# Joining small TensorE products in the head loop of a hybrid transformer layer

## The chip, the cores and the metric

One Trainium2 chip, one core of it. The metric is the time of one execution of the whole program on the device, in microseconds (us); of several runs the median is given. One layer is computed, with all of its weights read from HBM.

## The reference, cut to what matters

The change lies in the three attention-like mixers. For 256 tokens and 8 heads of 128 channels the reference computes:

```python
proj = rms_norm(x) @ w_in                      # q, k, v of three mixers, gates
# A: sliding window with sinks ("sw")
scores = einsum('qd,kd->qk', q, k) * d ** -0.5      # over the window
e = exp(scores - max(scores, sink)); probs = e / (sum(e) + exp(sink - m))
out_a = probs @ v
# B: stick breaking ("sb")
z = q @ k.T
a = exp(log_sigmoid(z) + between)              # between: a reverse cumulative sum
out_b = a @ v
# C: gated DeltaNet ("dn"), chunks of 64
n_mat = -strict_lower(kbeta @ k.T * decay)
t_mat = eye + n_mat; power = n_mat
for _ in range(5):
    power = power @ power
    t_mat = t_mat + t_mat @ power
```

Behind it come gated sums of the three, an output product, a mixture of 32 experts and a gated input embedding.

## The kernel before, in words

**Dense work.** Every weight matrix is split into a high and a low part of type fp32r, and each product is the sum of three: high by high, high by low, low by high. In the head stage a tile of 128 columns of the input projection is 48 matmuls (`tile`, L494, its matmul is L509); `dense` (L532) runs a quarter of it, 12 matmuls. ScalarE (ACT) makes the high part (`hi`), VectorE (DVE, `lo`, L1349, recorded as L1352) the low part of even tiles and GpSimd (POOL, `lo_pieces`, L459, four pieces each, recorded as L463) that of odd tiles, once ACT has made the high part.

**Heads.** `mix` is written once for each engine (TensorE: PE, L542; ACT, L1089; DVE, L1438) and runs for heads 1 to 8. It interleaves the small fp32 products of head n with 32 pieces of dense work, which are head n+1's projection (in head 8: the first gate products, fp32r matmuls of 512 columns, L713). Between two pieces stands one group of small products; the program order on each engine is written out by hand, and semaphores tie the engines. The groups that matter here, all on PE:

- L554 `dn_ss`, then one dense piece, then L558 `sw_ss` (a sum of squares over the channels for the sliding window's q), which waits for `dn_rt`, ACT's reading of the L554 result in the same bank; two dense pieces; then L564 and L565 `sb_z` (stick-breaking scores).
- L587 and L588 `sw_s` (sliding window scores) behind dense(9); L592 to L594 `sb_arg` (stick-breaking cumulative sums) behind dense(10); L599 `dn_p` behind dense(11).
- L604 `sw_prT` (three transposes of the sliding window's probabilities) behind dense(12).
- rounds r = 0 to 5 of the matrix power (L613 to L618 and L623, products of 64 by 64 blocks), one behind each of dense(13) to dense(18); the last matmul of that dense piece is held until DVE's `dn_round` and ACT's `dn_roundp` of the round before. Behind round 0 stands `sw_av` (L628, L629), behind round 1 `sb_av` (L634, L635), the products of probabilities and values.

ACT between them: `sw_rt` after `hi(2)`; three exponentials after `sw_max`; `Exp` of `am` after `sb_amin`; `evac(2)`; copies of `dn_p` into `pm` and `n21`; the copy of `sw_prT` into `pT`; `hi(5)`; then the copies of the rounds. DVE: the scan for `sb_sp` (L1463, L1466), the sliding window's mask and maximum (L1470 to L1475, gives `sw_max`), the decayed products and `dn_round` (L1479 to L1489), the cap of `sb_arg` (L1491, `sb_amin`), the normalization (L1493 to L1498, `sw_pr`), `lo(4)`, then for each round the copies L1503 and L1505 (`dn_round`), and behind rounds 0 to 3 a tap of head n+1's convolution (`next_tap`: L1423, a copy of 12 columns, and three instructions at L1428 in the first tap, L1430 in the others). Head 8 has no taps and no POOL work, and its `lo(3)` is a real subtraction (L1547); in heads 1 to 7 `lo(3)` is empty.

Of the kernel before, what the change touches and what calls it, by code (L numbers as in the profile page):

```python
# [18 lines left out]
ALU = mybir.AluOpType  # L19
# [63 lines left out]
def hybrid_trunk(nc, x, p, mix_norm, w_in, swa_q_norm, swa_k_norm, swa_sinks, sb_q_norm, sb_k_norm, dn_conv,  # L83
# [3 lines left out]
    with ctx:  # L87
# [28 lines left out]
        def event(name, n):  # L116

            name, before = base.get(name, (name, 0))
            return sem(name), n + before
# [355 lines left out]
        def _(pe):  # L475
# [66 lines left out]
            def mix(m, n, dense):  # L542
# [5 lines left out]
                for t in range(TT):  # L548
# [5 lines left out]
                mm(bank[5][:], ones[:], sq_dn, start=True, stop=True).then_inc(sem("dn_ss"), 1)  # L554
                dense(5)
                pe.wait_ge(*event("dn_rt", n))
                pe.wait_ge(*event("sw_sq", n))
                mm(bank[5][:, 0:S], ones[:], sq_sw, start=True, stop=True).then_inc(sem("sw_ss"), 1)  # L558
                dense(6)
                dense(7)  # L560

                pe.wait_ge(*event("sb_qk", n))
                kk = qk_sb[:, S:2 * S]
                mm(bank[3][:, 0:S], kk[:, 0:P], qk_sb[:, 0:S], start=True, stop=False, skip_group_check=True)  # L564
                mm(bank[3][:, S:S + P], kk[:, P:S], qk_sb[:, P:S], start=False, stop=False, skip_group_check=True)\  # L565
                    .then_inc(sem("sb_z"), 1)
                dense(8)

# [14 lines left out]
                dense(9)  # L583

                pe.wait_ge(*event("sw_q", n))
                kT = kT_sw[:, ds(m // 4, 1), :].rearrange("p a s -> p (a s)")
                mm(bank[4][:, 0:P], q_sw[:, 0:P], kT[:, 0:P], start=True, stop=True)  # L587
                mm(bank[4][:, P:3 * P], q_sw[:, P:S], kT[:, 0:S], start=True, stop=True).then_inc(sem("sw_s"), 1)  # L588
                dense(10)

                pe.wait_ge(*event("sb_sp", n))
# [9 lines left out]
                dense(12)  # L601
                pe.wait_ge(*event("sw_pr", n))
                for b in range(3):
                    m_ = pe.transpose(bank[4][:, b * P:b * P + P], smx[:, b * P:b * P + P], ident[:])  # L604
                m_.then_inc(sem("sw_prT"), 1)

                for r in range(6):
# [16 lines left out]
                    m_.then_inc(sem("dn_sqr"), 1)  # L624
                    if r == 0:
                        pe.wait_ge(*event("sw_pT", n))
                        pe.wait_ge(*event("sb_v", n))
                        mm(bank[2][:, 0:S], v_sw[:, 0:P], pT[:, 0:S], start=True, stop=False, skip_group_check=True)  # L628
                        mm(bank[2][:, P:S], v_sw[:, P:S], pT[:, S:3 * P], start=False, stop=True, skip_group_check=True)\  # L629
                            .then_inc(sem("sw_av"), 1)  # L630
                    if r == 1:
                        pe.wait_ge(*event("sb_a", n))
                        pe.wait_ge(*event("sw_out", n))
                        mm(bank[2][:, S:2 * S], v_sb[:, 0, :], am[:, 0:S], start=True, stop=False, skip_group_check=True)  # L634
                        mm(bank[2][:, S + P:2 * S], v_sb[:, 1, :], am[:, S:3 * P], start=False, stop=True,  # L635
                           skip_group_check=True).then_inc(sem("sb_av"), 1)
# [372 lines left out]
        def _(act):  # L1009
# [79 lines left out]
            def mix(n, evac, hi, sigmoid_conv):  # L1089
# [49 lines left out]
                f(n21[BLOCKS[1], :, :], nT_psum[BLOCKS[1], :, 0:CH], ACT.Copy).then_inc(sem("dn_n21"), 1)  # L1139
                act.wait_ge(*event("sw_prT", n))  # L1140
                f(pT, bank[4][:, 0:384], ACT.Copy).then_inc(sem("sw_pT"), 1)
                hi(5)
                for r in range(5):
                    act.wait_ge(*event("dn_sqr", 6 * n - 5 + r))
                    f(pm, pm_psum, ACT.Copy).then_inc(sem("dn_roundp"), 1)
                    if r == 0:
                        act.wait_ge(*event("sw_av", n))
                        f(outs[:, 0, ds(n - 1, 1), :].rearrange("p a s -> p (a s)"), bank[2][:, 0:S], ACT.Copy)\
                            .then_inc(sem("sw_out"), 1)
                    if r == 3:  # L1150
# [4 lines left out]
                    if r == 2:  # L1155
                        evac(3)
                        act.wait_ge(*event("sb_av", n))
                        f(outs[:, 1, ds(n - 1, 1), :].rearrange("p a s -> p (a s)"), bank[2][:, S:2 * S], ACT.Copy)\
                            .then_inc(sem("sb_out"), 1)
# [160 lines left out]
        def _(dve):  # L1320
            tt, ts, stt = dve.tensor_tensor, dve.tensor_scalar, dve.scalar_tensor_tensor

            def nxt():

                dve.drain()  # L1325
# [112 lines left out]
            def mix(n, next_tap, next_silu, lo):  # L1438
# [29 lines left out]

                dve.wait_ge(*event("sw_s", n))
                tt(smx, bank[4][:, 0:384], masksw[:].rearrange("p b n -> p (b n)"), ALU.add)  # L1470
                nxt()
                dve.tensor_reduce(sm[:, 0:1], smx[:, 0:P], AX.X, ALU.max)
                dve.tensor_reduce(sm[:, 1:2], smx[:, P:3 * P], AX.X, ALU.max)
                nxt()
                ts(sm[:, 2:4], sm[:, 0:2], hs[:, F_SINK:F_SINK + 1], -1.0, ALU.max, ALU.mult).then_inc(sem("sw_max"), 1)  # L1475

                dve.wait_ge(*event("dn_dec", n))
# [10 lines left out]
                dve.wait_ge(*event("dn_eg", n))  # L1488
                tt(eG, eG, qk_dn[:, P:S], ALU.mult).then_inc(sem("decays_used"), 1)  # L1489
                dve.wait_ge(*event("sb_arg", n))  # L1490
                tt(am, bank[3][:, 0:384], capsb[:].rearrange("p b n -> p (b n)"), ALU.min).then_inc(sem("sb_amin"), 1)  # L1491
# [341 lines left out]
```

## Time and profile before

| | us |
|---|---|
| median of 3 runs | 2133.97 |
| lowest and highest | 2130.94, 2138.09 |
| the profiled execution's own time | 2128.3 |
| its span in the trace | 2126.6 |
| PE busy in the span | 1796.1 (84%) |
| DVE, ACT, POOL busy | 864.0, 691.1, 191.2 |
| mean granted TensorE clock | 0.944 |

The profiled execution is one run with the profiler on; its span runs from the first to the last instruction in the trace. A busy PE is not PE at its peak, since the records of pipelined matmuls overlap: a matmul's record is longer than the distance to the next one's start, so distances between starts tell what a piece costs.

### The profile page before, as it was taken

To read this page: it belongs to the slowest core of one execution; us is meant where nothing else is said; L and a number is where in the kernel's file an instruction comes from. 1 tells how busy PE (TensorE), PEld (TensorE's weight loads), DVE (VectorE), ACT (ScalarE), POOL (GpSimd) and SP (SyncE) were. 2 spreads that over 40 slices of the span, in tenths; PEclk is the share of its full clock that TensorE was granted. 3 is DMA by queue.
4 is the path that set the end of the run, shared out by engine and by line. 5 is a ranking of instruction groups with operands and counts; after the bars stand their busy time and mean duration, and the time that the engine had idled before them with its cause. 6 is when DMAs were issued, how large, how long until landed. Compare 5 with 4: busy or idle time off the path is not lost.

```text
span 2126.6 us, 42236 instructions
## 1 busy us (share of the span) xinstructions
PE 1796.1 (84%) x17850; PEld 1354.2 (64%) x17851; DVE 864.0 (41%) x1392; ACT 691.1 (32%) x954; POOL 191.2 (9%) x167
## 2 busy tenths in 40 slices
PE   7999999999999999998977776666666666666699
PEld 7899999999878888887753443333333333333477
DVE  4555445554464445444433332222222222222274
ACT  4466655566654434333320111100011010110173
POOL 3433233223100000000000000000000000000000
PEclk9999999999999999999989998888888999988899
DMA  9555545454445555556759999999999999999972
GB/s 180 152 134 138 133 126 135 119 137 128 131 157 191 186 197 191 188 195 240 279 208 426 425 425 427 427 425 425 427 428 427 426 425 427 427 426 426 425 279 87
DMA packets 258914, 593.01 MB, mean 279 GB/s; under 512 B 31530, under 2 KB 171050, under 8 KB 225322
## 3 DMA queue, kind: packets, MB, share of 16 engines
q1 hardware_dynamic: 258858, 592.19, 74.7%
q8 instruction: 43, 0.70, 0.1%
q14 instruction: 13, 0.11, 0.0%
HBM read 590.07 MB, written 2.10 MB: 278 GB/s over the span
## 4 chain that ended last, share of the span: by engine, by line
PE 58%; DMA 34%; ACT 3%; DVE 2%; issue 1%; DVEq 1%; ACTq 1%; SPq 0%
DMA ring<-in_w_e_down 33%; PE bank L713 22%; PE bank L509 16%; PE bank L899 5%; PE bank L957 4%; PE bank L872 2%; ACT ring L1011 1%; PE bank L616 1%; ACT L1011 1%; PE bank L858 1%; PE bank L918 1%; PE bank L849 1%; DVEq L1325 1%; DMA ring<-in_w_out 0%; ACT wh L1011 0%
## 5 line engine op out<-in xcount | busy, mean ns | idle before, releaser
L1011 ACT ACTIVATE wh<-ring 128x2048 fp32r<-128x2048 f32 x156 | 298.3, 1913 | 218.9 <-DMA ring<-in_w_in 99.3
L872 PE MATMUL bank<-ring,mo 128*32 128x128 f32 x6144 | 216.4, 301 | 134.0 <-DMA ring<-in_w_e_up 114.1
L1011 ACT ACTIVATE mo<-bank 128x128 f32<-128x128 f32 (+5 forms) x232 | 72.5, 323 | 711.9 <-PE bank L886 308.9
L872 PEld LDWEIGHTS bank<-ring,mo 128*32 128x32 f32 x6144 | 187.8, 121 | 177.7 <-DMA ring<-in_w_e_up 143.7
L1547 DVE TENSOR_TENSOR wl<-ring,wh 128x2048 fp32r<-128x2048 f32 x86 | 197.0, 2292 | 218.2 <-ACT wh L1011 218.2
L899 PE MATMUL bank<-ring,mo 128*32 128x512 f32 x1024 | 163.5, 768 | 93.1 <-DMA ring<-in_w_e_down 87.3
L463 POOL TENSOR_TENSOR wl<-ring,wh 128x512 fp32r<-128x512 f32 x132 | 171.7, 1333 | 342.9 <-ACT wh L1011 342.9
L509 PE MATMUL bank<-xh,wh 128*128 128x256 f32 x1088 | 162.4, 296 | 3.0 <-ACT xh L1011 3.0
L1715 DVE TENSOR_TENSOR x_tok<-x_tok,bank 128x512 f32<-128x512 f32 x256 | 158.3, 680 | 0.0
L509 PE MATMUL bank<-xl,wh 128*128 128x256 f32 x1088 | 154.1, 289 | 0.0
L899 PEld LDWEIGHTS bank<-ring,mo 128*32 128x32 f32 x1024 | 33.8, 125 | 187.0 <-DMA ring<-in_w_e_down 97.1
L509 PE MATMUL bank<-xh,wl 128*128 128x256 f32 x1088 | 149.0, 286 | 2.5 <-DVE wl L1352 2.5
L509 PEld LDWEIGHTS bank<-xh,wh 128*128 128x128 f32 x1088 | 139.7, 193 | 11.4 <-issue 5.7
L509 PEld LDWEIGHTS bank<-xl,wh 128*128 128x128 f32 x1088 | 139.9, 193 | 1.2
L509 PEld LDWEIGHTS bank<-xh,wl 128*128 128x128 f32 x1088 | 137.1, 191 | 5.3 <-DVE wl L1352 2.9
L1725 DVE COPY mo<-bank 128x512 f32<-128x512 f32 x32 | 22.1, 692 | 242.2 <-PE bank L858 242.2
L1739 DVE TENSOR_TENSOR mo<-mo,bank 128x128 f32<-128x128 f32 x32 | 9.2, 288 | 269.1 <-PE bank L872 269.1
L1011 ACT ACTIVATE raw_dn<-bank 128x512 f32<-128x512 f32 (+1 forms) x56 | 28.0, 500 | 255.3 <-PE bank L899 248.6
L1011 ACT ACT_TABLE_LOAD x66 | 84.7, 1283 | 48.1 <-issue 43.1
L713 PE MATMUL bank<-wh,xh 128*128 128x512 f32 x384 | 97.2, 392 | 0.0
L713 PE MATMUL bank<-wl,xh 128*128 128x512 f32 x384 | 96.8, 391 | 0.0
L713 PE MATMUL bank<-wh,xl 128*128 128x512 f32 x384 | 96.7, 392 | 0.0
(354 smaller groups left out, 2350.4 us busy)
## 6 DMA issues: line engine op xcount, KB each, us to landing
ring<-in_w_e_down SPq DMA_DIRECT2D x64, 2048.0 KB, 26.2
ring<-in_w_e_up SPq DMA_DIRECT2D x64, 2048.0 KB, 26.2
ring<-in_w_in SPq DMA_DIRECT2D x116, 1024.0 KB, 5.5
ring<-in_w_e_gate SPq DMA_DIRECT2D x32, 2048.0 KB, 30.3
xnT<-in_w_e_gate SPq DMA_DIRECT2D x16, 2048.0 KB, 29.6
mo<-in_w_e_gate SPq DMA_DIRECT2D x16, 2048.0 KB, 33.9
ring<-in_w_out SPq DMA_DIRECT2D x16, 1024.0 KB, 5.2
ring<-in_w_ple_gate SPq DMA_DIRECT2D x8, 2048.0 KB, 15.1
```

The source lines that it names most:

```text
L463: i = pool.tensor_tensor(wl[p][:, k:k + 4, :], slot[p][:, k:k + 4, :], wh[p][:, k:k + 4, :], ALU.subtract)
L509: m = mm(to, w_[:, k, :], x_[:, k, :], start=(i == 0), stop=(i == len(steps) - 1))
L616: m_ = mm(pow_psum[rows_, t, :, :], pm[rows_, t, :], powT[rows_, t, :, :], start=True, stop=True)
L713: m = mm(to[t][:], x_(k0 + k, t), w_[p][:, k, :], start=(first and j < 8 and k == 0), stop=(last and j >= 16 and k == 3))
L849: m = mm(bank[4 + j][:], swT[32 * j:32 * j + 32, t, :], ysb[32 * j:32 * j + 32, :], start=True, stop=True)
L872: m = mm(bank[b][32 * j:32 * j + 32, 0:P], xw[:, 8 * (i % 2) + k, :], m_gu[piece][:, k, j * P:j * P + P], start=(i % 2 == 0 and k == 0), s ...
L899: m = mm(bank[3][32 * j:32 * j + 32, :], hT[:, 32 * c:32 * c + 32], m_down[i][:, 0, a, j * 512:j * 512 + 512], start=(c == 0), stop=(c == 3))
L957: m = mm(bank[ACC_BANK[u // 2] + t][:], x_[:, 8 * (u % 2) + k, t * P:t * P + P], w_[:, k, :], start=(first and k == 0), stop=(last and k = ...
L1011: return act.activation(out, in_, func, **kw)
L1547: tt(ul[u % PAIRS], unit_slot[u % PAIRS], uh[u % PAIRS], ALU.subtract).then_inc(sem("u_lo"), 1)
L1715: i = tt(o, o, bank[4 + j][:], ALU.add)
L1725: dve.tensor_copy(xg, bank[0][:]).then_inc(sem("xg"), 1)
```

## The change

It moves four of the small groups so that each stands directly beside another one, with no dense piece between, and moves what consumes them on ACT and DVE: `sw_ss` stands one dense piece later, `sb_z` one earlier, together; `sw_s` stands one dense piece later, in front of `sb_arg`; `sw_prT` moves from behind dense(12) to behind round 0; `sw_av` moves from behind round 0 to behind round 1, in front of `sb_av`. The wait for `sw_out` goes, both outputs are copied behind round 2, and the second product of the shared bank has `start=False`. On DVE the mask and maximum move behind the decayed products. Nothing is computed otherwise than before.

```diff
@@ -553,17 +553,16 @@
                 pe.wait_ge(*event("sb_rt", n))
                 mm(bank[5][:], ones[:], sq_dn, start=True, stop=True).then_inc(sem("dn_ss"), 1)
                 dense(5)
+                dense(6)
                 pe.wait_ge(*event("dn_rt", n))
                 pe.wait_ge(*event("sw_sq", n))
                 mm(bank[5][:, 0:S], ones[:], sq_sw, start=True, stop=True).then_inc(sem("sw_ss"), 1)
-                dense(6)
-                dense(7)
-
                 pe.wait_ge(*event("sb_qk", n))
                 kk = qk_sb[:, S:2 * S]
                 mm(bank[3][:, 0:S], kk[:, 0:P], qk_sb[:, 0:S], start=True, stop=False, skip_group_check=True)
                 mm(bank[3][:, S:S + P], kk[:, P:S], qk_sb[:, P:S], start=False, stop=False, skip_group_check=True)\
                     .then_inc(sem("sb_z"), 1)
+                dense(7)
                 dense(8)
 
                 pe.wait_ge(*event("dn_qk", n))
@@ -582,12 +581,12 @@
                 m_.then_inc(sem("dn_kk"), 1)
                 dense(9)
 
+                dense(10)
+
                 pe.wait_ge(*event("sw_q", n))
                 kT = kT_sw[:, ds(m // 4, 1), :].rearrange("p a s -> p (a s)")
                 mm(bank[4][:, 0:P], q_sw[:, 0:P], kT[:, 0:P], start=True, stop=True)
                 mm(bank[4][:, P:3 * P], q_sw[:, P:S], kT[:, 0:S], start=True, stop=True).then_inc(sem("sw_s"), 1)
-                dense(10)
-
                 pe.wait_ge(*event("sb_sp", n))
                 mm(bank[3][:, 0:S], negL[:], sp[:, 0:S], start=False, stop=False, skip_group_check=True)
                 mm(bank[3][:, P:S], nones[:], sp[:, S:S + P], start=False, stop=False, skip_group_check=True)
@@ -599,11 +598,6 @@
                     m_ = pe.transpose(nT_psum[:, t, :], nT[:, t, :], ident[:])
                 m_.then_inc(sem("dn_p"), 1)
                 dense(12)
-                pe.wait_ge(*event("sw_pr", n))
-                for b in range(3):
-                    m_ = pe.transpose(bank[4][:, b * P:b * P + P], smx[:, b * P:b * P + P], ident[:])
-                m_.then_inc(sem("sw_prT"), 1)
-
                 for r in range(6):
                     dense(13 + r, lambda: (pe.wait_ge(*event("dn_round", 6 * n - 5 + r)),
                                            pe.wait_ge(*event("dn_roundp", 6 * n - 5 + r))))
@@ -623,15 +617,18 @@
                                 m_ = mm(pm_psum[rows_, t, :], w_, pm[rows_, t, :], start=True, stop=True)
                     m_.then_inc(sem("dn_sqr"), 1)
                     if r == 0:
+                        pe.wait_ge(*event("sw_pr", n))
+                        for b in range(3):
+                            m_ = pe.transpose(bank[4][:, b * P:b * P + P], smx[:, b * P:b * P + P], ident[:])
+                        m_.then_inc(sem("sw_prT"), 1)
+                    if r == 1:
                         pe.wait_ge(*event("sw_pT", n))
                         pe.wait_ge(*event("sb_v", n))
                         mm(bank[2][:, 0:S], v_sw[:, 0:P], pT[:, 0:S], start=True, stop=False, skip_group_check=True)
                         mm(bank[2][:, P:S], v_sw[:, P:S], pT[:, S:3 * P], start=False, stop=True, skip_group_check=True)\
                             .then_inc(sem("sw_av"), 1)
-                    if r == 1:
                         pe.wait_ge(*event("sb_a", n))
-                        pe.wait_ge(*event("sw_out", n))
-                        mm(bank[2][:, S:2 * S], v_sb[:, 0, :], am[:, 0:S], start=True, stop=False, skip_group_check=True)
+                        mm(bank[2][:, S:2 * S], v_sb[:, 0, :], am[:, 0:S], start=False, stop=False, skip_group_check=True)
                         mm(bank[2][:, S + P:2 * S], v_sb[:, 1, :], am[:, S:3 * P], start=False, stop=True,
                            skip_group_check=True).then_inc(sem("sb_av"), 1)
                 dense(19, lambda: (pe.wait_ge(*event("dn_T", n)), pe.wait_ge(*event("dn_n21", n))))
@@ -1137,16 +1134,13 @@
                 f(pm[BLOCKS[0], :, :], nT_psum[BLOCKS[0], :, 0:CH], ACT.Copy)
                 f(pm[BLOCKS[1], :, :], nT_psum[BLOCKS[1], :, CH:P], ACT.Copy).then_inc(sem("dn_roundp"), 1)
                 f(n21[BLOCKS[1], :, :], nT_psum[BLOCKS[1], :, 0:CH], ACT.Copy).then_inc(sem("dn_n21"), 1)
-                act.wait_ge(*event("sw_prT", n))
-                f(pT, bank[4][:, 0:384], ACT.Copy).then_inc(sem("sw_pT"), 1)
                 hi(5)
                 for r in range(5):
                     act.wait_ge(*event("dn_sqr", 6 * n - 5 + r))
                     f(pm, pm_psum, ACT.Copy).then_inc(sem("dn_roundp"), 1)
                     if r == 0:
-                        act.wait_ge(*event("sw_av", n))
-                        f(outs[:, 0, ds(n - 1, 1), :].rearrange("p a s -> p (a s)"), bank[2][:, 0:S], ACT.Copy)\
-                            .then_inc(sem("sw_out"), 1)
+                        act.wait_ge(*event("sw_prT", n))
+                        f(pT, bank[4][:, 0:384], ACT.Copy).then_inc(sem("sw_pT"), 1)
                     if r == 3:
                         hi(6)
                     if r == 4:
@@ -1155,6 +1149,7 @@
                     if r == 2:
                         evac(3)
                         act.wait_ge(*event("sb_av", n))
+                        f(outs[:, 0, ds(n - 1, 1), :].rearrange("p a s -> p (a s)"), bank[2][:, 0:S], ACT.Copy)
                         f(outs[:, 1, ds(n - 1, 1), :].rearrange("p a s -> p (a s)"), bank[2][:, S:2 * S], ACT.Copy)\
                             .then_inc(sem("sb_out"), 1)
                 act.wait_ge(*event("dn_y", n))
@@ -1466,14 +1461,6 @@
                 tt(spd, spd, bc(upper[:].unsqueeze(1), [P, 2, P]), ALU.mult).then_inc(sem("sb_sp"), 1)
                 lo(3)
 
-                dve.wait_ge(*event("sw_s", n))
-                tt(smx, bank[4][:, 0:384], masksw[:].rearrange("p b n -> p (b n)"), ALU.add)
-                nxt()
-                dve.tensor_reduce(sm[:, 0:1], smx[:, 0:P], AX.X, ALU.max)
-                dve.tensor_reduce(sm[:, 1:2], smx[:, P:3 * P], AX.X, ALU.max)
-                nxt()
-                ts(sm[:, 2:4], sm[:, 0:2], hs[:, F_SINK:F_SINK + 1], -1.0, ALU.max, ALU.mult).then_inc(sem("sw_max"), 1)
-
                 dve.wait_ge(*event("dn_dec", n))
                 dve.wait_ge(*event("dn_kk", n))
                 tt(attnT, bank[7][:, S:2 * S], decT, ALU.mult)
@@ -1487,6 +1474,14 @@
                        bc(ident[rows_, CH * i:CH * i + CH].unsqueeze(1), [CH, TT, CH]), ALU.add)
                 dve.wait_ge(*event("dn_eg", n))
                 tt(eG, eG, qk_dn[:, P:S], ALU.mult).then_inc(sem("decays_used"), 1)
+                dve.wait_ge(*event("sw_s", n))
+                tt(smx, bank[4][:, 0:384], masksw[:].rearrange("p b n -> p (b n)"), ALU.add)
+                nxt()
+                dve.tensor_reduce(sm[:, 0:1], smx[:, 0:P], AX.X, ALU.max)
+                dve.tensor_reduce(sm[:, 1:2], smx[:, P:3 * P], AX.X, ALU.max)
+                nxt()
+                ts(sm[:, 2:4], sm[:, 0:2], hs[:, F_SINK:F_SINK + 1], -1.0, ALU.max, ALU.mult).then_inc(sem("sw_max"), 1)
+
                 dve.wait_ge(*event("sb_arg", n))
                 tt(am, bank[3][:, 0:384], capsb[:].rearrange("p b n -> p (b n)"), ALU.min).then_inc(sem("sb_amin"), 1)
                 dve.wait_ge(*event("sw_exp", n))
```

## Rows read from the trace of the kernel before

**Rows 1.** The page: the span, and the chain that ended last, by engine.
```profile
span 2126.6 us, 42236 instructions
PE 58%; DMA 34%; ACT 3%; DVE 2%; issue 1%; DVEq 1%; ACTq 1%; SPq 0%
```

**Rows 2.** The same chain in order of time: start, length (us), what.
```profile
182.07 1.11 PE bank L554 x2
...
246.37 1.11 PE bank L554 x2
```

**Rows 3.** Timeline of PE, head 3: start, length (us), instructions merged.
```profile
247.78 1.11 PE L509 MATMUL bank<-xl,wh 128*128 128x256 f32 x8
249.01 0.70 PE L558 MATMUL bank<-ring,ones 128*128 128x256 f32 x2
...
259.35 0.59 PE L592 MATMUL bank<-ring,negL 128*128 128x256 f32 x2
...
261.66 0.38 PE L599 MATMUL bank<-ident,mo 128*128 128x128 f32 x2
...
265.26 0.45 PE L613 MATMUL bank<-mo 64*64 64x64 f32 x8
...
268.15 0.65 PE L616 MATMUL bank<-mo 64*64 64x128 f32 x8
...
271.25 0.65 PE L616 MATMUL bank<-mo 64*64 64x128 f32 x8
...
273.69 0.65 PE L616 MATMUL bank<-mo 64*64 64x128 f32 x8
```

**Rows 4.** Timeline of ACT, head 3.
```profile
259.71 0.40 ACT L1011 ACTIVATE ring<-ring,sm 128x128 f32<-128x128 f32 x1 [0.86 <-DVE sm L1475]
...
260.60 0.28 ACT L1011 ACTIVATE sm<-sm,hs 128x2 f32<-128x2 f32 x1
262.41 0.53 ACT L1011 ACTIVATE ring<-ring 128x384 f32<-128x384 f32 x1 [1.53 <-DVE ring L1491]
...
264.33 1.91 ACT L1011 ACTIVATE wh<-ring 128x2048 fp32r<-128x2048 f32 x1
```

**Rows 5.** Timeline of DVE, head 3.
```profile
258.12 0.56 DVE L1470 TENSOR_TENSOR ring<-bank,masksw 128x384 f32<-128x384 f32 x1 [1.52 <-PE bank L588]
...
259.58 0.42 DVE L1479 TENSOR_TENSOR ring<-bank,ring 128x256 f32<-128x256 f32 x1
...
261.82 0.55 DVE L1491 TENSOR_TENSOR ring<-bank,capsb 128x384 f32<-128x384 f32 x1
262.29 0.15 DVE L1493 TENSOR_TENSOR sm<-sm 128x2 f32<-128x2 f32 x1
...
263.22 2.28 DVE L1352 TENSOR_TENSOR wl<-ring,wh 128x2048 fp32r<-128x2048 f32 x1
...
266.21 0.17 DVE L1423 COPY hc<-head 128x12 f32 x1
266.46 3.85 DVE L1428 TENSOR_SCALAR ring<-raw_dn,hc 128x256 f32<-128x256 f32 x3
...
270.43 0.28 DVE L1505 TENSOR_TENSOR mo<-bank,mo 128x128 f32<-128x128 f32 x1
```

**Rows 6.** Timeline of POOL, head 3.
```profile
266.31 5.14 POOL L463 TENSOR_TENSOR wl<-ring,wh 128x512 fp32r<-128x512 f32 x4 [7.30 <-ACT wh L1011]
```

**Rows 7.** Timeline of POOL and DVE ahead of head 1: the first tap there.
```profile
92.71 5.16 POOL L463 TENSOR_TENSOR wl<-ring,wh 128x512 fp32r<-128x512 f32 x4 [9.40 <-ACT wh L1011]
...
93.10 0.93 DVE L1423 COPY hc<-head 128x12 f32<-128x12 f32 x1
```

**Rows 8.** Timeline, head 8: DVE, then PE.
```profile
576.76 2.28 DVE L1547 TENSOR_TENSOR wl<-ring,wh 128x2048 fp32r<-128x2048 f32 x1
...
585.97 0.45 PE L613 MATMUL bank<-mo 64*64 64x64 f32 x8
```

**Rows 9.** Timeline ahead of head 1: a DVE subtraction beside POOL's.
```profile
68.33 3.38 DVE L1352 TENSOR_TENSOR wl<-ring,wh 128x2048 fp32r<-128x2048 f32 x1
```

## The prediction

> **What bounds the kernel now.** I read the page first. The span is 2126.6 us, and on the chain that ended last PE has 58% and DMA 34% [rows 1]. The chain in order of time is next: from head to head it runs through PE, and the product `dn_ss` comes back every 64.3 us (246.37 - 182.07) [rows 2]. Between its end and its return the chain leaves PE once only, where PE runs dry behind dense(4) while ACT finishes the head before. That detour begins when PE's own last dense piece ends, so it moves with PE, and what PE saves in a head is saved in the time. It is handed on to the experts as well, whose loads wait for slots that PE's products free.
>
> Then the timelines of one head, engine by engine. A dense matmul has a pitch of 0.12 us (eight in 1.11 with a last record of 0.28) [rows 3], so a piece of 12 takes 1.44. The first thing to see is what a small group costs. From `sb_arg` at 259.35 to `dn_p` at 261.66 are 2.31 us, one piece and 0.87 for 512 fp32 columns, or 0.22 for 128 of them. From round 1 to round 2 are 3.10 us, from round 2 to round 3 2.44; the 0.66 between them is `sb_av`'s 384 columns at the same price [rows 3]. So a group costs its columns and no more, whether a dense piece or another group stands before it. **In heads 1 to 7 going from 22 groups to 19 is by itself worth nothing.** What can be won is waiting.
>
> **The change, part by part, heads 1 to 7.**
>
> *`sw_ss` later.* The dense matmuls ahead of it are issued by 248.74 (247.78 + 8 x 0.12); it starts at 249.01, 0.27 late, and its two records take 0.70 where the unwaited pair of L592 takes 0.59, so the wait costs 0.27 + 0.11 = 0.38 us [rows 3]. One dense piece later `dn_rt` is long there. Its consumer on ACT comes behind `hi(2)`, and is about 0.2 late; DVE has 1.52 us of slack before L1470 [rows 5], which covers it. `sb_z` moved ahead needs `sb_qk`, ready before: nothing. Gain 0.38.
>
> *`sw_prT` out of its place.* From `dn_p` to round 0 are 3.60 us [rows 3]: two pieces 2.88, `dn_p`'s two transposes 0.22, the three of `sw_prT` 0.33, 0.09 of switching to 64-row blocks, which every round has, and 0.08 to 0.1 left, a wait for `sw_pr`. Behind round 0 the 0.33 is paid again and the wait is not. Gain 0.1.
>
> *`sw_s` later, the maximum moved behind the decayed products.* What is late next: ACT's exponentials stand in front of the copies that round 0 waits for. With PE 0.38 ahead, `sw_s` starts at 258.35 where `sb_arg` now starts less 0.65 and 0.38, and ends about 1.08 later than before, so L1470 runs at 259.2 instead of 258.12. ACT's first exponential follows at 1.59 as now (259.71 - 258.12) [rows 4, 5]: 260.8, the third at 261.7. By then `sb_arg` is capped, and the `Exp` of `am` comes at 261.9, ahead of today's 262.41 [rows 4]. The rest of ACT up to `hi(5)` now takes 1.9 us, 0.5 of it waiting for and copying `pT`, which leaves that place: 1.4, so the copies for round 0 are there at 263.1, round 0 asks at 264.3. Hidden, with 1.2 us to spare. `hi(5)` starts at 263.3 and ends at 265.2, and POOL starts at 265.25, 1.06 earlier than now [rows 6].
>
> *The first tap.* DVE normalizes once the third exponential has ended, 261.96, and `lo(4)` follows 0.93 later as now (263.22 - 262.29) [rows 5]: 262.9 to 265.2. Round 0 starts at about 264.5, its copy runs at 265.24, the copy of 12 columns (L1423) at 265.46. Now this last one runs at 266.21, 0.1 ahead of POOL's first piece at 266.31, and takes 0.17 [rows 5, 6]. In the changed kernel POOL has begun 0.2 before it. The trace has that case: ahead of head 1 POOL starts at 92.71, L1423 at 93.10, and it takes 0.93 instead of 0.17: it ends with POOL's piece [rows 7]. The three instructions behind it also end with one piece each, 3.85 us for three that meet three boundaries [rows 5]. With the copy on the first boundary the tap ends when all four pieces have: POOL's 5.14 and 0.15, at 265.25 + 5.3 = 270.5; L1505 then ends at 270.9, where today it ends at 270.71 [rows 5].
>
> The Trainium skill (GPSIMD Engine Reference, Key points) says that GpSimd shares its SBUF interfaces with VectorE and that instructions with two SBUF inputs meet it as well. By that `lo(4)`, which has two, would be drawn into it too and the time be that of rival C.
>
> *Rounds 0 to 2 on PE.* Unhindered, round 0 is at 264.5, round 1 at +2.89 - 0.65 + 0.33 = 267.1, round 2 at +3.10 + 0.65 = 270.8, 0.45 ahead of 271.25 [rows 3]. The held matmul stands 0.2 before it, at 270.6, and is now served at 270.95: a wait of 0.35 to 0.45 that does not exist today (270.71 is 0.3 before today's 271.04). That gives nearly all of it back. **Per head 0.48 - 0.43 = 0.05 us; seven heads 0.35.** Its bounds are 0.48 (no block) and -0.1 (the block plus another exposed weight load).
>
> *Moved behind it.* `sw_av` needs `pT`, copied by 266.2 and asked for at 267.9; one copy more behind round 2 meets ACT idle; the wait for `sw_out` that goes was never last. Nothing for these, and no DMA moves.
>
> **Head 8** has neither tap nor POOL. There DVE is late: its subtraction runs from 576.76 to 579.02 [rows 8], and dn_p and round 0 both wait behind it. In the new order the decayed products follow at once, 2.24 us (261.82 - 259.58) [rows 5], L1470 at 581.2, the first exponential at 582.8, the `Exp` of `am` at 583.9, the copies at 584.8, round 0 at 585.1 instead of 585.97 [rows 8]: 0.9, less 0.33 for the transposes that now stand behind it: 0.5 us. Ends: 0 and 1.1.
>
> **Sum:** 0.35 + 0.5 = 0.9 us. The profiled execution took 2128.3, so 2127.4; against the median of 2133.97, 2133.1 us. A measurement of this kernel can tell about 0.3%, 6.4 us, from no change.
>
> **The rivals.**
>
> *A. The copy of 12 columns gets in ahead of POOL.* It misses by 0.2 us in sums with errors of about 0.1. Then each head keeps 0.48: 7 x 0.48 + 0.5 = 3.9 us, 2130.1. Chance 0.25, also "same".
>
> *B. A switch has a price that joining saves.* Against it speaks the 0.87 and the 0.66. The largest leftover beside a group is 0.1 to 0.2 (0.11 at L558). With 0.15 for each of three joins in eight heads, 3.6, and case A on top, 7.5 us, 2126.5. Chance 0.07, faster.
>
> *C. Slower: `lo(4)` overlaps POOL's pieces.* Its end at 265.2 and POOL's start at 265.25 are a near tie. Ahead of head 1 a DVE subtraction beside POOL took 3.38 instead of 2.28 [rows 9, 5], so round 0's copy and the tap are 1.1 late or more. It decides once POOL starts over 0.5 us inside `lo(4)`. Round 2 would wait 0.4 + 1.1: 7 x (0.48 - 1.5) + 0.5 = 6.6 us slower, 2140.6. 0.05 us of overlap, by these sums, buys next to nothing. Chance 0.06. The rule of the Trainium skill named above (GPSIMD Engine Reference, Key points) would be its mechanism; the 3.38 agrees with it.
>
> *D. The change does not do what it says*: the joined groups would still be separated. The diff leaves no dense piece between them, so this has no chance worth a number.
>
> **How the numbers follow.** My forecast has 0.57, A 0.25, B 0.07, C 0.06; 0.05 is left for what spreads on both sides. The runs before alone lie between 2130.94 and 2138.09, so the range takes in A and some spread on either side: 2128 to 2138. Faster by over 0.3% 0.09, slower 0.07, within 0.84.
>
> **What would show it.** In head 3 of the changed trace: `sw_ss` without a wait; `sw_prT` behind round 0 without one; L1470 some 1.1 us later and round 0 some 0.75 earlier; POOL 1.06 earlier against the same start of the head; L1423 near 0.9 to 1 us instead of 0.17; and a new wait of PE behind DVE's L1505 ahead of round 2. Heads 64.2 to 64.3 us apart would bear it out, 63.8 rival A. It is wrong if the heads come closer by more than 0.5 us, or if POOL and `lo(4)` lengthen each other.

## The result, and the profile after

Over 15 runs of each, the changed kernel has a median of 2136.98 us, the kernel before 2132.83; the ratio is 1.002, with a 95% interval of 1.0012 to 1.0029. (Single runs of 2482.4 and 5919.59 us lie among them; the ratio leaves disturbed runs out.) **The change costs 4 us, some 0.2%.** That is within the 0.3% that I had called "same" and within the range, but clear of noise and on the other side of my 0.9 us gain. The profiled execution has 2136.55 us and a span of 2134.8.

The page of the changed kernel: the span, and the chain that ended last, by engine.

```profile
span 2134.8 us, 42228 instructions
PE 50%; DMA 34%; ACT 5%; DVE 5%; DVEq 3%; issue 2%; ACTq 1%; POOL 0%; SPq 0%; POOLq 0%
```

PE's share of the chain fell from 58% to 50%, and DVE, with 2% in [rows 1], has 5% and its sequencer 3. The waits of PE in the part that holds heads 2 to 7 (from 180 to 560 us), total, times, longest, before and after:

```profile
PE bank L554 <- ACT ring L1011: 5.1, 6, 0.8
```

```profile
PE bank L509 <- DVE mo L1500: 6.4, 6, 1.1
PE bank L554 <- ACT ring L1008: 5.0, 6, 0.8
```

One wait is new, six times 1.1 us: the held dense matmul ahead of round 2 waits for `dn_round` (L1500 is L1505 of before). The wait at `dn_ss` is what it was. The chain of the changed kernel in head 2 shows the way to it (start, length, what; dots stand for steps left out):

```profile
183.12 1.10 PE bank L554 x2
...
187.56 0.47 ACT ring L1008
...
192.46 0.56 DVE ring L1458
...
194.35 0.60 DVE mo L1469
195.05 1.19 DVE mo L1473
196.84 0.47 DVE ring L1478
198.34 0.50 ACT ring L1008 x3
200.57 1.46 DVE wl L1347
...
202.97 1.17 DVE hc L1418
...
206.78 1.29 DVE ring L1423
208.90 0.58 PE bank L610 x8
...
248.25 1.10 PE bank L554 x2
```

Before, the chain from head to head was PE and the detour behind dense(4). Now it also leaves PE for over 20 us, from `sw_rt` on ACT over DVE's scan, decayed products, identity adds, maximum, normalization, `lo(4)` and the tap, and comes back in round 2. `dn_ss` returns after 65.13 us (248.25 - 183.12), where it was 64.3 [rows 2].

The same places as [rows 3 to 6], in head 3 of the changed kernel, where `dn_ss` starts at 248.25 instead of 246.37, so 1.88 is to be taken off for a comparison. PE:

```profile
252.05 0.59 PE L559 MATMUL bank<-ring,ones 128*128 128x256 f32 x2
252.48 0.59 PE L562 MATMUL bank<-ring 128*128 128x256 f32 x2
...
266.35 0.45 PE L607 MATMUL bank<-mo 64*64 64x64 f32 x8
...
268.86 0.65 PE L610 MATMUL bank<-mo 64*64 64x128 f32 x8
...
271.01 1.56 PE L509 MATMUL bank<-xh,wl 128*128 128x256 f32 x11
273.63 0.38 PE L509 MATMUL bank<-xh,wl 128*128 128x256 f32 x1 [1.06 <-DVE mo L1500]
273.94 0.65 PE L610 MATMUL bank<-mo 64*64 64x128 f32 x8
```

DVE and POOL:

```profile
255.79 5.42 POOL L463 TENSOR_TENSOR wl<-ring,wh 128x512 fp32r<-128x512 f32 x4 [15.56 <-ACT wh L1008]
...
260.17 1.49 DVE L1473 TENSOR_TENSOR mo<-mo,ident 64x128 f32<-64x128 f32 x2
...
261.88 0.55 DVE L1478 TENSOR_TENSOR ring<-bank,masksw 128x384 f32<-128x384 f32 x1
...
267.94 5.08 POOL L463 TENSOR_TENSOR wl<-ring,wh 128x512 fp32r<-128x512 f32 x4 [6.73 <-ACT wh L1008]
268.01 1.25 DVE L1418 COPY hc<-head 128x12 f32 x1
269.34 3.84 DVE L1423 TENSOR_SCALAR ring<-raw_dn,hc 128x256 f32<-128x256 f32 x3
```

Four things are to be seen. `sw_ss` (L559) has 0.59 for its pair, so it no longer waits. Round 1 and round 2 (both L610) start 5.08 us apart (268.86 and 273.94), where [rows 3] and the 0.65 for the moved `sw_av` make 3.75: so the new wait costs 1.33 us from start to start. The 1.06 beside it counts only from the end of the record before. The two identity adds (L1473) take 1.49 us together. And the copy of 12 columns starts 0.07 behind POOL and takes 1.25 instead of 0.17. The line of the adds over all heads, before and then after (durations of one in ns: shortest, median, longest):

```profile
L1486 DVE TENSOR_TENSOR mo<-mo,ident x16: 282/286/290, 132.4 to 582.1; 64x128 f32<-64x128 f32 x16
```

```profile
L1473 DVE TENSOR_TENSOR mo<-mo,ident x16: 284/291/1193, 129.9 to 586.6; 64x128 f32<-64x128 f32 x16
```

### The profile page after: what moved, and what is told of

The parts are those of the page before. It is cut to its first block, busy times and chain, and to the rows that moved or that the text cites. A ratio compares the mean times of both kernels' runs of the same rounds, so it can differ in the third digit from the quotient of the medians.

```text
span 2134.8 us, 42228 instructions
## 1 busy us (share of the span) xinstructions
PE 1791.8 (84%) x17850; PEld 1351.2 (63%) x17851; DVE 875.1 (41%) x1392; ACT 691.0 (32%) x954; POOL 191.8 (9%) x167
## 4 chain that ended last, share of the span: by engine, by line
PE 50%; DMA 34%; ACT 5%; DVE 5%; DVEq 3%; issue 2%; ACTq 1%; POOL 0%; SPq 0%; POOLq 0%
DMA ring<-in_w_e_down 33%; PE bank L710 21%; PE bank L509 11%; PE bank L896 4%; PE bank L954 4%; DVEq L1320 2%; PE bank L869 2%; ACT ring L1008 2%; ACT wh L1008 1%; PE bank L855 1%; ACT L1008 1%; DVE wl L1347 1%; PE bank L610 1%; PE bank L915 1%; DVE ring L1423 1%
## 5 line engine op out<-in xcount | busy, mean ns | idle before, releaser
L509 PE MATMUL bank<-xl,wh 128*128 128x256 f32 x1088 | 148.2, 285 | 0.0
```

The lines of the kernel that those rows point to most:

```text
L509: m = mm(to, w_[:, k, :], x_[:, k, :], start=(i == 0), stop=(i == len(steps) - 1))
```

## The experiments

The theory after this reading: some of DVE's instructions on SBUF operands are held until the piece that POOL is in ends (which ones, the last section sorts). This bites twice in the changed kernel, at the identity adds and at the 12-column copy, and each time a little work costs up to a piece of 1.3 us. The rival: POOL has no share, the DVE and ACT chain is simply too long behind scores that come later.

Distances between heads are read as the start of the `dn_ss` product in head 7 less that in head 2, by five. They repeat within 0.04 us from head to head, far better than the time of a run, which spreads over some 8 us. Compare the ratios, not the times: each goes by the runs of the kernel before that stood beside it. All runs:

| kernel | start in head 2, head 7 | apart | time, us | ratio (95%) |
|---|---|---|---|---|
| before | 182.08, 503.57 | 64.30 | 2132.83 | |
| changed | 183.12, 508.73 | 65.12 | 2136.98 | 1.002 (1.0012 to 1.0029) |
| changed, early copy | 181.44, 500.87 | 63.89 | 2129.03 | 0.9991 (0.9982 to 1.0) |
| changed, late adds | 182.33, 504.00 | 64.33 | 2130.30 | 0.9999 (0.9989 to 1.001) |
| changed, both | 183.78, 502.79 | 63.80 | 2127.00 | 0.999 (0.9981 to 0.9999) |
| changed, POOL held | 184.27, 515.18 | 66.18 | 2144.63 | one run |
| before, part 1 | 182.46, 502.14 | 63.94 | 2130.87 | 1.0003 (0.9991 to 1.0014) |
| before, part 3 | 181.74, 502.54 | 64.16 | 2131.48 | one run |
| before, DVE's order | 184.55, 507.91 | 64.67 | 2135.72 | one run |
| before, early copy | 182.19, 503.70 | 64.30 | 2132.14 | one run |
| before, parts 1 and 3 | 181.39, 500.37 | 63.80 | 2126.57 | 0.9979 (0.9969 to 0.9989) |
| the same, early copy | 180.57, 499.55 | 63.80 | 2126.42 | 0.9975 (0.9966 to 0.9984) |
| that and dense(5) first | 182.98, 499.70 | 63.34 | 2126.75 | 0.9977 (0.9966 to 0.9988) |

The kernel before, run beside them, had medians of 2130.92 us (beside the changed kernel with either edit and with both, and part 1), 2132.92 (POOL held, part 3, DVE's order, and parts 1 and 3 with the early copy), 2131.51 (early copy alone, dense(5) first) and 2131.85 (parts 1 and 3). Parts 1 and 3 together ran on two occasions; the other had one time, 2129.24, and the same distance.

### Each of the two holds taken away

*The early copy.* On DVE, in the changed kernel (written out here; the same two lines go from behind round 0, and head 8, which has no taps, gets none):

```diff
                 ts(smx[:, P:3 * P], ...).then_inc(sem("sw_pr"), 1)
+                dve.wait_ge(*event("raw", 8 * (n + 1) - 5))
+                dve.tensor_copy(hc[:], head[:, F_CONV:NF, ds(n, 1)]...)
                 lo(4)
```

> The changed kernel, with the 12-column copy of the next head's tap weights moved on DVE from behind round 0 to ahead of lo(4). Theory (DVE instructions that take the SBUF interface that POOL uses end only with one of POOL's pieces): in the changed kernel this copy took 1.25 us instead of 0.17 and used up the first of four boundaries, so without it the tap meets three, L1500's partner ends about 1.1 us earlier, PE's wait ahead of round 2 falls from 1.06 to 0.2 us or less, and heads come 64.0 us apart instead of 65.1: some 7 us off, 2130. Rival (the wait comes only of DVE and ACT running late behind the later scores, POOL has no share): the copy costs its 0.2 us wherever it stands, heads stay 65.1 to 65.3 us apart and the time 2137.

Measured: 63.89 us apart, ratio 0.9991. DVE and POOL in head 3 of it:

```profile
257.27 1.50 DVE L1477 TENSOR_TENSOR mo<-mo,ident 64x128 f32<-64x128 f32 x2
...
262.71 0.17 DVE L1416 COPY hc<-head 128x12 f32 x1
262.79 2.29 DVE L1347 TENSOR_TENSOR wl<-ring,wh 128x2048 fp32r<-128x2048 f32 x1
...
265.05 5.13 POOL L463 TENSOR_TENSOR wl<-ring,wh 128x512 fp32r<-128x512 f32 x4 [6.73 <-ACT wh L1008]
265.38 3.66 DVE L1427 TENSOR_SCALAR ring<-raw_dn,hc 128x256 f32<-128x256 f32 x3
```

The copy takes 0.17, the adds are still slow, and the tap, which starts 0.33 behind POOL, ends at 269.04, with POOL's third piece instead of behind its last. A copy of 12 columns cost 1.23 us a head by its place. The rival falls, since nothing else in the chain was shortened.

*The late adds.*

```diff
                 tt(nT, ...).then_inc(sem("dn_round"), 1)
-                for i, rows_ in enumerate(BLOCKS):
-                    tt(powT[rows_, :, 1, :], nT[rows_, ...], bc(ident[rows_, ...]), ALU.add)
-                dve.wait_ge(*event("dn_eg", n))
-                tt(eG, eG, qk_dn[:, P:S], ALU.mult).then_inc(sem("decays_used"), 1)
                 dve.wait_ge(*event("sw_s", n))
...
                 tt(am, bank[3][:, 0:384], ...).then_inc(sem("sb_amin"), 1)
+                for i, rows_ in enumerate(BLOCKS):
+                    tt(powT[rows_, :, 1, :], nT[rows_, ...], bc(ident[rows_, ...]), ALU.add)
+                dve.wait_ge(*event("dn_eg", n))
+                tt(eG, eG, qk_dn[:, P:S], ALU.mult).then_inc(sem("decays_used"), 1)
```

> The changed kernel, with the two adds of the identity (powT) and the product with the decays moved behind the maximum and the cap on DVE. Theory (the first of these adds took 1.19 us instead of 0.28 because it ran beside POOL's last piece of the part before): the mask and maximum start as soon as the scores are there, 0.8 us earlier, the adds take 0.28 each since POOL has ended, and all that follows up to round 2 comes 0.7 to 0.8 us earlier: wait ahead of round 2 about 0.3 us, heads 64.3 to 64.4 us apart, 2132. Rival (the adds are slow wherever they stand, or the order of DVE is not what matters): adds still near 1.2 us, heads 65 or more apart.

Measured: 64.33 apart. In head 3 of it:

```profile
259.50 0.56 DVE L1472 TENSOR_TENSOR ring<-bank,masksw 128x384 f32<-128x384 f32 x1 [0.98 <-PE bank L589]
...
261.43 0.57 DVE L1482 TENSOR_TENSOR mo<-mo,ident 64x128 f32<-64x128 f32 x2
...
265.58 5.10 POOL L463 TENSOR_TENSOR wl<-ring,wh 128x512 fp32r<-128x512 f32 x4 [5.92 <-ACT wh L1008]
265.74 1.16 DVE L1418 COPY hc<-head 128x12 f32 x1
...
271.28 0.38 PE L509 MATMUL bank<-xh,wl 128*128 128x256 f32 x1 [0.28 <-DVE mo L1499]
```

The adds take 0.57 behind POOL's run, the mask now waits for the scores, the copy is still held, and PE's new wait is 0.28. This edit also takes the adds out of the path, so by itself it doesn't tell their slowness from their place; the kernel with POOL held does that, below. An estimate from the rows of the changed kernel says the same: with 0.58 instead of 1.49 for the adds, the decayed products would end at 261.96 - 0.91 = 261.05, just as the scores do (261.03), so the new order alone would have cost next to nothing. With the scores as the last thing that the mask waits for and only the copy held, my forecast was 0.05 us less than 64.30 a head, and 64.33 is measured: near it.

*Both.*

> Both edits on the changed kernel. Theory: no wait left ahead of round 2, and what joining was worth by the forecast is seen: heads 63.8 us apart, 0.48 less than in the kernel before; with some 0.5 us of head 8, 2129. It would beat both kernels. Rival (late chain alone): no better than one of the two edits, 64.3 or more.

Measured: 63.80 apart, 0.50 less than before, where 0.48 was forecast for a head with no hold; ratio 0.999. The heads would make more of it in time: 7 x 0.50 = 3.5 us and 1.1 in head 8, where the ratio gives 2.1 (0.2 to 4.0). The two edits alone gave 1.23 and 0.79, together 1.32: they shorten one chain, and what PE waits for can be taken away only once.

### POOL's share alone

In the changed kernel, on POOL:

```diff
                 for s in range(1, 8, 2):
+                    if s == 3:
+                        pool.wait_ge(*event("decays_used", h))
                     lo_pieces(s % PAIRS, 8 * h + s + PRO)
```

> The changed kernel, with POOL made to wait before its part of the third tile until DVE has done the identity adds and the product with the decays. Theory: the first add falls from 1.19 to 0.28 us and the mask starts with the scores, 0.8 us earlier. But POOL's four pieces then lie beside DVE's normalization and lo(4): the scalar multiplications (L1492, L1493) take up to 1.3 us each, or lo(4) takes over 3 us, so heads are not closer than 64.8. Rival (the add is slow for a reason of its own, such as 64 partitions or the broadcast identity): it stays at 1.19.

Measured: 66.18 apart. In head 3 of it:

```profile
262.20 0.59 DVE L1475 TENSOR_TENSOR mo<-mo,ident 64x128 f32<-64x128 f32 x2
...
263.26 5.05 POOL L463 TENSOR_TENSOR wl<-ring,wh 128x512 fp32r<-128x512 f32 x4 [20.82 <-ACT wh L1010]
...
264.61 1.20 DVE L1485 TENSOR_SCALAR sm<-sm,hs 128x2 f32<-128x2 f32 x1
...
267.05 1.27 DVE L1490 TENSOR_TENSOR sm<-sm 128x2 f32<-128x2 f32 x1 [0.79 <-ACT sm L1010]
...
271.50 1.04 DVE L1420 COPY hc<-head 128x12 f32 x1
```

Same adds, same place in DVE's order, no POOL beside them: 0.59 instead of 1.49. So the slowness is POOL's. And the hold moved on to whatever lies beside POOL now, but not where I had expected it. POOL's four pieces had ended (263.26 + 5.05 = 268.31) before the scalar multiplications and `lo(4)` ran, which kept their time, while two instructions on two columns, of 0.23 and 0.15 us in the kernel before, took 1.20 and 1.27, and PE waited twice a head (1.3 and 0.6 at the longest).

### The parts of the change, one by one, on the kernel before

*Part 1, `sw_ss` beside `sb_z`.* The first hunk of the change alone:

```diff
                 dense(5)
+                dense(6)
                 pe.wait_ge(*event("dn_rt", n))
                 pe.wait_ge(*event("sw_sq", n))
                 mm(bank[5][:, 0:S], ones[:], sq_sw, ...).then_inc(sem("sw_ss"), 1)
-                dense(6)
-                dense(7)
...
                     .then_inc(sem("sb_z"), 1)
+                dense(7)
                 dense(8)
```

> The kernel before, with the first join alone: sw_ss one dense piece later beside sb_z one earlier. Theory: PE's wait of 0.27 us ahead of sw_ss and 0.11 of exposed weight load go, ACT's slack covers its later sum: heads 63.9 us apart instead of 64.3, 2.7 us off over seven heads, 2130. Rival (something behind takes it back): 64.3, no change. If joining saved a switch of engine state beside the wait, heads would be closer than 63.8.

Measured: 63.94 apart, 0.36 less. The time does not show it (1.0003, where 7 x 0.36 = 2.5 us would be 0.9988, just outside the interval): in the profiled run `dn_ss` of head 1 starts at 118.5 instead of 117.8, the last `dn_oss` at 619.99 instead of 621.80, and from there to the end of the span are 1507.6 us instead of 1504.8. Such differences outside the heads are in all the traces (behind the last `dn_oss` from 1504.8 to 1510.1 us, in no order that goes with the edits), and I have no reason for them.

*Part 3, `sw_prT` behind round 0, both value products behind round 1,* with ACT's copies as in the change:

```diff
-                pe.wait_ge(*event("sw_pr", n))
-                for b in range(3):
-                    m_ = pe.transpose(bank[4][:, b * P:b * P + P], ...)
-                m_.then_inc(sem("sw_prT"), 1)
...
                     if r == 0:
+                        pe.wait_ge(*event("sw_pr", n))
+                        for b in range(3):
+                            m_ = pe.transpose(bank[4][:, b * P:b * P + P], ...)
+                        m_.then_inc(sem("sw_prT"), 1)
+                    if r == 1:
                         pe.wait_ge(*event("sw_pT", n))
```

> The kernel before, with the third part alone: the transposes of the probabilities behind round 0 and both value products behind round 1. Theory: PE saves 0.1 us; ACT reaches hi(5) 0.5 us earlier, POOL starts at the time of the 12-column copy, and either the copy is in first and heads are 64.2 us apart, or it is caught, takes about 1.2 us, and a wait ahead of round 2 of 0.3 to 0.6 us makes them 64.5 to 64.8. Rival: POOL has no share, 64.2 in any case.

Measured: 64.16 apart, 0.14 less. In head 3 the copy is in ahead of POOL by 0.03 us, and takes 0.17:

```profile
265.32 0.17 DVE L1419 COPY hc<-head 128x12 f32 x1
265.35 5.15 POOL L463 TENSOR_TENSOR wl<-ring,wh 128x512 fp32r<-128x512 f32 x4 [6.82 <-ACT wh L1009]
```

*DVE's order alone,* the last two hunks:

```diff
-                dve.wait_ge(*event("sw_s", n))
-                tt(smx, bank[4][:, 0:384], ...)
...
                 tt(eG, eG, qk_dn[:, P:S], ALU.mult).then_inc(sem("decays_used"), 1)
+                dve.wait_ge(*event("sw_s", n))
+                tt(smx, bank[4][:, 0:384], ...)
...
                 dve.wait_ge(*event("sb_arg", n))
```

> The kernel before, with the order of DVE alone changed (mask and maximum behind the decayed products), PE and ACT as before. Theory: the decayed products now run while POOL makes the low part of the third tile, the first identity add takes 1.2 us instead of 0.28, the maximum comes 1.8 to 1.9 us later than before, and PE, which asks for the probabilities behind dense(12) as before, waits about 1.5 us for them: heads 65.6 to 65.9 us apart. Rival (no contention, only the order): the maximum 1.0 us later, wait 0.7 us, heads 65.0.

Measured: 64.67 apart, a wait of 0.3 us for the probabilities behind dense(12). The adds take 1.51 together, as the theory has it, and the mask comes 1.74 later. But both expectations had the wait too large. I had made the probabilities as late as the maximum; in the old order the decayed products stand between the maximum and the normalization and are 2.24 us of it, and in the new order only ACT's exponentials are.

*Parts 1 and 3, with and without the early copy:* the diffs of both parts, and that of the early copy.

> The kernel before, with the first and third part of the change and the 12-column copy ahead of lo(4), but with scores, cumulative sums and DVE's order as before (20 groups). Theory: joining as such is worth nothing in heads 1 to 7, only waits are; both are gone here too, so heads come 63.8 us apart, as with all parts and both edits, and the time is about 2128 where before is 2131. Rival (each join saves a switch): more than 63.8, by the missing join, about 63.9 to 64.0.

> First and third part of the change without the early copy. With the copy in its old place it falls within 0.1 us of POOL's start. Theory: if it is caught by POOL it takes about 1.2 us and heads are 64.0 to 64.3 us apart, against 63.80 with the early copy; if it is in first, 63.8. Either way length of the copy and distance of the heads go together.

> The first and third part alone once more, timed: with heads 63.80 us apart and head 8 shorter by 0.8 us, 3.5 + 0.8 = 4.3 us off the time before (ratio 0.998), the same as with the early copy within the spread. Rival (the early copy gives something beyond the distance of the heads, since with it the ratio was 0.9975): no better than 0.999.

Measured: 63.80 apart in all three traces, ratios 0.9975 and 0.9979, whose intervals cover each other. 63.80 is also what all parts give with both edits, so the join that is missing here (`sw_s` with `sb_arg`) is worth nothing in heads 1 to 7. Head 8 is 0.78 us shorter than before (62.93 between the last two `dn_oss`, against 63.71), where 0.8 was expected: 7 x 0.50 + 0.78 = 4.3 us, and the ratios give 4.5 and 5.3. Without the early copy the copy is ahead of POOL by 0.03 us (264.42 and 264.45 in head 3), which is luck of the schedule; with it there is no tie to win. **Two of the three joins, without the one that turns DVE's order round, beat both kernels.**

*The control:* the diff of the early copy on the kernel before.

> The kernel before with the 12-column copy ahead of lo(4) and nothing else: the control. Theory: there the copy is 0.1 us ahead of POOL and takes 0.17 us, nothing waits for the tap, so heads stay 64.3 us apart. Rival (the earlier copy is a gain of its own, whatever the change does): heads 64.1 or less.

Measured: 64.30 apart. The early copy has no gain of its own.

### One step further

```diff
                 dense(4)
+                dense(5)
                 pe.wait_ge(*event("dn_sq", n))
                 pe.wait_ge(*event("sb_rt", n))
                 mm(bank[5][:], ones[:], sq_dn, ...).then_inc(sem("dn_ss"), 1)
-                dense(5)
                 dense(6)
```

> A step further on the best kernel so far (first and third part and the early copy): one more dense piece ahead of dn_ss, where PE waits 1.0 us in every head for ACT. Theory: the wait of 1.0 goes, sw_ss is asked for 1.44 us earlier against dn_rt and waits 0.3 to 0.4 again; ACT's chain is 0.4 us later and its slack of 1.0 us ahead of the scores covers it: heads 63.2 us apart, 4 us more off. Rival (the chain from ACT to round 0 and the tap has no slack left): what PE gains at dn_ss it loses ahead of round 2, heads 63.8.

Measured: 63.34 apart, so 0.46 off each of them and not 0.6, and no change of the time against the kernel that it stands on (0.9977 to 0.9975). PE in head 3 of it:

```profile
246.33 1.02 PE L555 MATMUL bank<-ring,ones 128*128 128x512 f32 x2
...
248.89 0.70 PE L559 MATMUL bank<-ring,ones 128*128 128x256 f32 x2
```

The wait at `dn_ss` is gone, `sw_ss` has its 0.70 again, the mark of a wait. From `dn_ss` of head 1 to the last `dn_oss` the profiled runs have 496.9 us (119.6 to 616.48) against 499.7 without the step (116.8 to 616.49), so the heads are 2.8 us shorter. But head 1 starts 2.8 us later, 0.4 of it by the step itself, and the part behind the heads is 1.1 us shorter. These are single traces; over the runs nothing is gained, and why stays open.

## Why the prediction was wrong

**What held.** PE bounds the heads, and a saving there is kept. Joining as such is worth nothing in heads 1 to 7: part 1 gave 0.36 where its wait was put at 0.38, part 3 gave 0.14 where 0.1 was forecast, and the join of `sw_s` with `sb_arg` nothing. The 12-column copy was held by POOL, as at head 1 [rows 7], and the wait it makes is where it was forecast, ahead of round 2. Alone, this hold cost 64.33 - 63.80 = 0.53 us, where 0.43 was forecast.

**The step that failed** is "*`sw_s` later, the maximum moved behind the decayed products*", where it puts L1470 at 259.2 as soon as `sw_s` is there. It took the 2.24 us of the decayed products from [rows 5], where they run from 259.58 on. POOL's part of the third tile has ended there. The change moves them 2.9 us forward (258.55 - 1.88 = 256.67), into that part, and the first identity add was held to its end: 1.49 us for the pair, not 0.58. The mask came at 261.88 - 1.88 = 260.0, 0.8 late, and from then on nothing had slack: exponentials, normalization, `lo(4)`, the copy, the tap. So the term of the sum that failed is the 0.43 for PE's new wait: from start to start it cost 1.33 (5.08 - 3.75), and 0.50 - 1.33 = -0.83 is the change of the distance (0.50 is what both edits together leave of the saving that I had put at 0.48). The sum per head was forecast at +0.05 and is 64.30 - 65.12 = -0.82; with the adds out of the way it is -0.03. Of the signs that I had named, round 0 came as forecast (266.35 - 1.88 = 264.47), but the mask 1.88 us later than before instead of 1.1, and POOL 0.25 earlier (267.94 - 1.88 = 266.06) instead of 1.06: the near tie of copy and POOL stayed, at a later time. I had seen the first tap held and asked what a moved POOL would collide with, but not what a moved DVE block would.

Over seven heads that is 5.7 us, and the heads end 5.9 us later (the last `dn_oss` product starts at 627.66 instead of 621.80). The time rose by 4.2, with an interval of 2.6 to 6.2 by the ratio.

**Head 8** was forecast at 0.5 us and gave 0.12 (627.66 - 564.06 = 63.60 between the last two `dn_oss` products, against 621.80 - 558.08 = 63.72). By then `dn_ss` is 5.98 us late, so round 0 started at 591.24 - 5.98 = 585.26, as forecast (585.1), but round 1 came 2.54 us behind it instead of 2.29. The forecast had ended at round 0. Behind it DVE's copy for round 1 now stood behind the subtraction of `lo(4)`:

```profile
590.81 2.28 DVE L1542 TENSOR_TENSOR wl<-ring,wh 128x2048 fp32r<-128x2048 f32 x1
593.01 0.28 DVE L1498 COPY mo<-bank 128x128 f32<-128x128 f32 x1
```

In the kernel before, the subtraction ended at 586.25 and the copy started at 586.70, with time to spare.

**The rivals.** A (the copy is in first) did not happen here, but does in both kernels with part 3 on the order of before, by 0.03 us. B (a switch has its price) is refuted for heads 1 to 7. C had the right sign and the right kind of cause, DVE beside POOL, but the wrong place: `lo(4)` did not overlap, and the block that did was not in it. Nor would a POOL that starts inside `lo(4)` lengthen it, as C has it: with POOL held back that happened, and `lo(4)` kept its 2.28 us while POOL's piece gave way (last section). C's chance of 0.06 was too low, since I had given one place to a mechanism that every moved DVE instruction can meet. The Trainium skill (GPSIMD Engine Reference, Key points) names instructions with two SBUF inputs beside those in a two-port mode; the identity add is of the first kind, and the traces agree: 1.19 us beside POOL, 0.28 without. I had applied that sentence to `lo(4)` alone.

## What to carry to other kernels

When a block moves on one engine, redo its durations at the new time: list what POOL does there, not only who waits for the result. A DVE instruction of 0.2 us on SBUF operands can cost 1.2 if it starts behind a POOL instruction, so such small ones belong ahead of POOL's start, and a tie of 0.1 us between the two is a cost to be designed out, not a number to be rounded. And before joining groups, measure from start to start what a group costs beside its columns; if nothing, only the waits count.

## What the runs showed of the hardware

- Held by POOL until the end of one of its pieces of about 1.3 us: a copy of 12 columns (0.17 to 1.25 us), an add of 64 by 128 with both inputs in SBUF (0.28 to 1.19), and instructions on two columns (to 1.20 and 1.27).
- Not held: instructions of DVE with an input in PSUM, and reductions of one SBUF tensor. The mask (L1478 and its like) took 0.55 to 0.56 both behind POOL's run and, with POOL held back, beside it. There the two reductions behind the mask also ran beside POOL and took their usual 0.29 and 0.41.
- It goes both ways: in these rows, whichever of the two started first kept its time, and the other took longer. In head 3 of the changed kernel DVE's L1461 (two SBUF inputs) starts as POOL's second piece ends, 0.06 us ahead of the third, which takes 1.52 us where the one before took 1.29. L1469 (two as well) starts inside that piece and takes 0.61, where it took 0.42 in the kernel before (L1482):

```profile
258.21 0.43 DVE L1461 TENSOR_TENSOR ring<-ring,upper 128x256 f32<-128x256 f32 x1
258.27 1.52 POOL L463 TENSOR_TENSOR wl<-ring,wh 128x512 fp32r<-128x512 f32 x1
...
259.47 0.61 DVE L1469 TENSOR_TENSOR mo<-ring,hp 128x256 f32<-128x256 f32 x1 [0.17 <-issue]
```

- With POOL held back, `lo(4)` starts 1.23 us ahead of a piece of POOL, and the piece waits:

```profile
269.10 2.28 DVE L1349 TENSOR_TENSOR wl<-ring,wh 128x2048 fp32r<-128x2048 f32 x1
...
270.33 2.19 POOL L463 TENSOR_TENSOR wl<-ring,wh 128x512 fp32r<-128x512 f32 x1 [2.03 <-ACT wh L1010]
```

- Between dense fp32r matmuls a group of fp32 products cost its columns, 0.22 us for 128, and a wait ahead of one 0.11 us more than the time waited [rows 3].
